# Keys turned by the DMA crossbar instead of TensorE, scores two slots behind the keys, sample states through ScalarE's queue

## What is computed

```python
def _retention(q, k, v, S0):            # chunks of 128 tokens
    ...
    def body(S, blk):
        qc, kc, vc = blk
        sc = jnp.einsum('bihd,bjhd->bhij', qc, kc) * decay
        o = (jnp.einsum('bhij,bjhv->bihv', sc, vc)
             + jnp.einsum('bihd,bhdv->bihv', qc, S) * q_dec[None, :, :, None])
        S = S * s_dec[None, :, None, None] + jnp.einsum('bjhd,bjhv->bhdv', kc * k_dec[None, :, :, None], vc)
        return S, o
...
def _layer(h, pos, S0, norm_g, w_in, w_out, ws, bs, ln_g, ln_b):
    xn = _rmsnorm(h, norm_g)
    proj = jnp.einsum('btd,de->bte', xn, w_in)
    q, k, v, g_r, u, v_g, g_g = jnp.split(proj, SPLITS, axis=-1)
    q = _rope(q.reshape(B, T, RET_HEADS, RET_DK), pos)
    k = _rope(k.reshape(B, T, RET_HEADS, RET_DK), pos) * (RET_DK ** -0.5)
    o, S = _retention(q, k, v, S0)
    o = o * lax.rsqrt(jnp.mean(o * o, axis=-1, keepdims=True) + EPS)
    o = o.reshape(B, T, RET_WIDTH).astype(h.dtype) * jax.nn.silu(g_r)
    ...
    m = u * s.astype(h.dtype) * jax.nn.silu(g_g)      # s: causal mix of the normed v_g in chunks of 128
    y = jnp.einsum('bte,ed->btd', jnp.concatenate([o, m], axis=-1), w_out)
    return h + y, S.astype(S0.dtype), vn
```

## Time and profile before

| | |
|---|---|
| median of 3 runs | 1146.09 us (1145.93 to 1146.74) |
| profiled execution, its own time | 1150.53 us |
| its span on the slowest core (core 7) | 1148.7 us |
| spans of all cores | 1139.2 to 1148.7 us |
| mean granted TensorE clock, cores | 0.998 to 0.999 of full speed |
| busy on core 7: PE, DVE, POOL, ACT | 1117.0, 789.0, 671.1, 635.7 us |
| chain that ended last, by engine | PE 90%, DMA 6%, issue, DVE, ACT and POOL 1% each |

### The profile page before, as it was taken

The page is one execution under the profiler, slowest core; times in us unless marked ns, Lnnn a source line. Parts: engine busy times, 40 slices in busy tenths (PEclk is TensorE's granted clock), DMA queues, the critical chain, the costliest instruction groups (busy, mean ns, idle before and its releaser), DMA issues.

```text
span 1148.7 us, 26973 instructions; the slowest of 8 cores (1139.2 to 1148.7 us)
## 1 busy us (share of the span) xinstructions
PE 1117.0 (97%) x8910; PEld 677.4 (59%) x8910; DVE 789.0 (69%) x1654; ACT 635.7 (55%) x1150; POOL 671.1 (58%) x704
## 2 busy tenths in 40 slices
PE   4999999999999999999989999999999999998997
PEld 2544566677667667545544446667667667664453
DVE  3775867777777777784574486777776777777854
ACT  3764856556556556524444487555555655662433
POOL 3267556667666666513476784666766766662332
PEclk9999999999999999999999999999999999999999
DMA  9831646546536555779680227346545546576553
GB/s 192 208 106 42 87 111 131 127 69 137 122 73 136 118 104 146 154 225 231 176 190 6 60 32 159 95 82 131 116 85 126 118 87 131 133 102 150 202 178 145
DMA packets 149720, 144.29 MB, mean 126 GB/s; under 512 B 46288, under 2 KB 119760, under 8 KB 149328
## 3 DMA queue, kind: packets, MB, share of 16 engines
q1 hardware_dynamic: 128320, 99.83, 31.2%
q0 software_dynamic: 21120, 42.48, 23.9%
q10 hardware_dynamic: 144, 0.26, 0.1%
HBM read 127.14 MB, written 44.24 MB: 149 GB/s over the span
## 4 chain that ended last, share of the span: by engine, by line
PE 90%; DMA 6%; issue 1%; DVE 1%; ACT 1%; POOL 1%; SPq 0%; DVEq 0%; ACTq 0%; POOLq 0%
PE ps L848 27%; PE ps L869 17%; PE ps L726 13%; PE ps L1292 13%; PE ps L657 4%; DMA cats<-catn 2%; PE ps L1228 2%; PE ps L949 1%; PE ps L1076 1%; PE ps L967 1%; PE ps L994 1%; PE ps L932 1%; DMA h<-hb_51 1%; PE ps L1034 1%; PE ps L997 1%
## 5 line engine op out<-in xcount | busy, mean ns | idle before, releaser
L848 PE MATMUL ps<-xnT,RW 128*128 128x512 bf16 x1536 | 359.6, 379 | 0.0
L848 PEld LDWEIGHTS ps<-xnT,RW 128*128 128x128 bf16 x1536 | 143.3, 98 | 141.4
L869 PE MATMUL ps<-RW,xnT 128*128 128x256 bf16 x1920 | 219.3, 272 | 0.0
L869 PEld LDWEIGHTS ps<-RW,xnT 128*128 128x128 bf16 x1920 | 184.1, 98 | 21.0
L897 POOL TENSOR_TENSOR kn<-A_k,B_k 128x512 bf16<-128x512 f32 x64 | 81.5, 1273 | 90.6 <-DVE B_k L893 52.8
L491 ACT ACT_TABLE_LOAD x73 | 93.7, 1283 | 44.7 <-DVE rs L1005 35.7
L491 ACT ACTIVATE B_q<-ps 64x512 f32<-64x512 f32 x128 | 75.8, 592 | 42.4 <-DVE A_q L906 36.7
L885 DVE SCALAR_TENSOR_TENSOR A_k<-ps,small,kr 128x256 f32<-128x256 f32 x128 | 56.1, 479 | 62.7 <-PE ps L869 52.5
L1015 POOL TENSOR_TENSOR catn<-og,rs 128x512 bf16<-128x512 f32 x64 | 66.0, 1045 | 41.6 <-ACT rs L491 31.1
L976 DVE SCALAR_TENSOR_TENSOR S_72<-S_72,ps 128x128 f32<-128x128 f32 x240 | 68.2, 284 | 17.4 <-DVE S_72 L976 2.9
L491 ACT ACTIVATE sgr_78<-ps 128x512 bf16<-128x512 f32 x32 | 19.1, 597 | 90.8 <-DVE B_k L893 87.1
(11 more groups left out here) (566 smaller groups left out, 2564.6 us busy)
## 6 DMA issues: line engine op xcount, KB each, us to landing
RW<-w_h POOLq DMA_DIRECT2D x80, 256.0 KB, 5.3
stt_124<-st SPq DMA_DIRECT2D x16, 512.0 KB, 5.2
stt_123<-st SPq DMA_DIRECT2D x16, 512.0 KB, 7.0
ss_out<-stt_123 SPq DMA_DIRECT2D x16, 512.0 KB, 4.1
ss_out<-stt_124 SPq DMA_DIRECT2D x16, 512.0 KB, 5.0
cats<-catn SPq DMA_DIRECT2D x28, 256.0 KB, 2.1
hb_49<-xp SPq DMA_DIRECT2D x6, 512.0 KB, 5.3
hb_50<-xp SPq DMA_DIRECT2D x6, 512.0 KB, 5.6
```

The source lines that it names most:

```text
L848: r = e.matmul(ps[:, b, :], w[:, k, :], xnT[:, k, s], start=(k == 0), stop=(k == 7))
L869: r = e.matmul(out(c).rearrange("p (g d) -> p g d", g=2), x, RW[:, 8 * sk + k:8 * sk + k + 9:8, :], start=(k == 0), stop=(k == 7))
```

## The change

The keys of units 0 to 30 in each layer (62 of 64) are no longer turned by PE. kn is written to DRAM (kd, 128 KB), from SP's queue, and a transposing DMA (the crossbar), also from SP, reads it into kT. The last unit of a layer keeps KT. kn and kT become two buffers each. SC and OO work for the unit two slots back, pp, and KV for the slot before, p. The gate's SiLU (GR) and the product for k32 (K32) become functions of their own. s32 takes the memory of sq. Of the state transfers, the loads for heads 1 to 7 and the stores for heads 0 to 6 are issued by ScalarE (28 and 28 in both layers), with slack 8.0 and 2.0. The turns of cats get a slack of 7.0 in all heads but the last. Behind the loop, the rest of units 30 and 31 is interleaved with the first products of the output projection. dma has a slack argument like dma_t's. The functions P_gg, P_q, P_u, GM and the sample group are otherwise as they were; KT, SC and KV index the two buffers by u.n % 2. DVE's and POOL's instructions are the same.

```diff
@@ Prog.schedule
-                free[e] = s + issue
+                free[e] = s + (0.4 if e == "act" else issue)
@@ build_nc
+    kd = nc.dram_tensor("kd", [H * NQ, 128, 512], BF16, kind="Internal").ap()
...
-        kT = T("kT", [128, 512], BF16)
-        kn = T("kn", [128, 4, 128], BF16)
+        kT = [T("kT%d" % i, [128, 512], BF16) for i in range(2)]
+        kn = [T("kn%d" % i, [128, 4, 128], BF16) for i in range(2)]
...
-        s32 = T("s32", [128, 512], F32)
+        s32 = T("s32", [128, 512], F32, at=sq.off)
...
+        LATER = 7.0
+
+        def dma_t(out, in_, r, w, key, nbytes, slack=0.0):
+            lastT[key] = i = P.add("sp", lambda e: e.dma_start_transpose(out=out, in_=in_), r, w, semkey=key, nbytes=2.5 * nbytes,
                                after=[lastT[key]] if key in lastT else ())
+            P.ops[i].slack = slack
@@ P_kgr
-            act(t[:].rearrange("p (c d) -> p c d", c=4), kg[:, :, 1, :], AF.Silu, [], t.k() + kb, 512, tset="silu")
-            pool(lambda e: e.tensor_tensor(out=kn[:], in0=a3, in1=b3, op=ALU.add), A_k.k() + B_k.k(), kn.k(), 512)
+            kn_ = kn[u.n % 2]
+            pool(lambda e: e.tensor_tensor(out=kn_[:], in0=a3, in1=b3, op=ALU.add), A_k.k() + B_k.k(), kn_.k(), 512)
+            if u.n < H * NQ - 1:
+                dma("sp", kd[u.n], kn_[:].rearrange("p c d -> p (c d)"), kn_.k(), [("kd", u.n)], kn_.name, 131072)
...
+        def GR(l, u):
...
+        def K_turn(l, u):
+            t = kT[u.n % 2]
+            dma_t(t[:].rearrange("p (c i) -> p c i", c=4), kd[u.n], [("kd", u.n)], t.k(), "kT", 131072)
+
         def KT(l, u):
...
+        def K32(l, u):
...
@@ OO
                 dma_t(VO[:, h, t0:t0 + n * 512].rearrange("p (c i) -> p c i", c=4 * n), src,
-                      names, VO.k(h, (t0, t0 + n * 512)), "catT", 131072 * n)
+                      names, VO.k(h, (t0, t0 + n * 512)), "catT", 131072 * n, LATER if h < H - 1 else 0.0)
@@ s_load
-            dma("sp", t[:], st_in[l, half * 8:half * 8 + 8, h].rearrange("b d v -> d b v"), [], t.k(), t.name, 524288, after=after)
+            dma("act" if h else "sp", t[:], st_in[l, half * 8:half * 8 + 8, h].rearrange("b d v -> d b v"), [], t.k(),
+                (t.name, "l", min(h, 1)), 524288, after=after, slack=8.0 if h else 0.0)
@@ s_kv
-                    dma("sp", ss_out[l, half * 8:half * 8 + 8, h].rearrange("b d v -> d b v"), t[:], t.k(), [("sso", l, h, half)], t.name, 524288)
+                    dma("act" if h < H - 1 else "sp", ss_out[l, half * 8:half * 8 + 8, h].rearrange("b d v -> d b v"), t[:], t.k(), [("sso", l, h, half)], (t.name, "s", h < H - 1), 524288, slack=2.0)
@@ the loop over units
+                if pp:
+                    SC(l, pp)
                 P_kgr(l, u)
+                P_gg(l, u)
+                if pp:
+                    OO(l, pp)
+                GR(l, u)
+                P_q(l, u)
                 if p:
-                    SC(l, p)
-                P_q(l, u)
+                    KV(l, p)
+                if u.q == 3:
+                    next(kv)
+                P_u(l, u)
                 if u.q == 3:
                     next(kv)
                 if p:
                     GM(l, p)
-                P_gg(l, u)
-                if p:
-                    OO(l, p, pp)
-                if u.q == 3:
-                    next(kv)
-                for f in (KT, P_u) if p else (P_u, KT):
-                    f(l, u)
+                if n < H * NQ - 1:
+                    K_turn(l, u)
+                if u.q == 0:
+                    K32(l, u)
...
-                KV(l, u)
@@ behind the loop
-            o_front(l, 0, 0, 4)
+            SC(l, pp)
+            KT(l, p)
+            GM(l, p)
+            o_front(l, 0, 0, 1)
+            OO(l, pp)
+            KV(l, p)
+            o_front(l, 0, 1, 2)
             SC(l, p)
-            GM(l, p)
-            OO(l, p, pp)
+            o_front(l, 0, 2, 4)
+            OO(l, p)
```

More of the change, by code:

```diff
@@ L498, in pool, with dma @@
             P.add("pool", fn, r, w, t_pool(n))
-        def dma(eng, out, in_, r, w, key, nbytes, after=(), **kw):
-            return P.add(eng, lambda e: e.dma_start(out=out, in_=in_, **kw), r, w, semkey=key, nbytes=nbytes, after=after)
+        def dma(eng, out, in_, r, w, key, nbytes, after=(), slack=0.0, **kw):
+            i = P.add(eng, lambda e: e.dma_start(out=out, in_=in_, **kw), r, w, semkey=key, nbytes=nbytes, after=after)
+            P.ops[i].slack = slack
+            return i
         lastT = {}
-        def dma_t(out, in_, r, w, key, nbytes):
-            lastT[key] = P.add("sp", lambda e: e.dma_start_transpose(out=out, in_=in_), r, w, semkey=key, nbytes=2.5 * nbytes,
+        LATER = 7.0
+        def dma_t(out, in_, r, w, key, nbytes, slack=0.0):
+            lastT[key] = i = P.add("sp", lambda e: e.dma_start_transpose(out=out, in_=in_), r, w, semkey=key, nbytes=2.5 * nbytes,
                                after=[lastT[key]] if key in lastT else ())
+            P.ops[i].slack = slack
         def ld(t, src, nbytes=65536, **kw):
@@ L858, in P_kgr @@
             w, w2 = W(l, u.h, "k"), W(l, u.h, "gr")
-            t = sgr[u.n % 2]
             kb = [bk(b) for b in KG]
@@ L900, in P_kgr @@
                      A_k.k() + B_k.k(), ra2.k(), 128)
+        def GR(l, u):
+            t = sgr[u.n % 2]
+            kg = ps[:, KG[0]:KG[1] + 1, :].rearrange("p b (c g d) -> p (b c) g d", c=2, g=2)
+            act(t[:].rearrange("p (c d) -> p c d", c=4), kg[:, :, 1, :], AF.Silu, [], t.k() + [bk(b) for b in KG], 512, tset="silu")
         def P_q(l, u):
@@ L931, in tr @@
                 for c in range(4):
-                    r = e.transpose(pb[:, c * 128:(c + 1) * 128], kn[:, c, :], identb[:])
+                    r = e.transpose(pb[:, c * 128:(c + 1) * 128], kn[u.n % 2][:, c, :], identb[:])
                 return r
[L934 to L939, removed]
+            pe(tr, kn[u.n % 2].k() + identb.k(), [bk(b)], 4 * SM)
+            t = kT[u.n % 2]
+            act(t[:], pb[:, 0:512], AF.Copy, [], t.k() + [bk(b)], 512)
+        def K32(l, u):
+            b2 = brot()
+            pe(lambda e: e.matmul(ps[:, b2, 0:32], ra2[:], identf[:, 0:32], start=True, stop=True), ra2.k() + identf.k(), [bk(b2)], 0.09)
+            dve(lambda e: e.tensor_copy(k32[:], ps[:, b2, 0:32]), [], k32.k() + [bk(b2)], 32)
         def SC(l, u):
             b = brot()
-            a, t, o = kT, qT[u.n % 2], scT
+            a, t, o = kT[u.n % 2], qT[u.n % 2], scT
             first = u.q == 0
@@ L960, in KV @@
             b = brot()
-            a = kn
+            a = kn[u.n % 2]
             h = u.h
@@ L982, in KV, with OO @@
             act(t[:], S32[:], AF.Copy, S32.k(), t.k(), 512)
-        def OO(l, u, prev):
+        def OO(l, u):
             b = brot()
@@ L1477, in build_nc @@
                 units.append(u)
-            tail_fill = []
             def slot(n):
```

## The result

The changed kernel takes 1198.37 us (median of 4 runs, 1194.85 to 1200.87), the kernel before 1146.41 in the same sessions: a ratio of 1.0449, 95% interval 1.042 to 1.0479, so 4.5% slower where 0.8% faster was forecast. The profiled execution's slowest core is again core 7.

The account below looks back on a forecast made before the run. PE was taken to bound the kernel, busy 1117.0 of 1148.7 us. The terms −13.6 + 2 + 2 = −9.6 us took the profiled 1150.5 to 1140.9, and 4.4 less for the median gave 1136.5 us, range 1131.0 to 1147.0.

Parts of the forecast that it names:

- PE, removed: On PE, 62 of 64 key transpositions go, at 0.22 us each: −13.6 us.
- Neither is on the path: On ACT, 37.1 us of copies removed and 20.7 us of state transfers added cost 0, ACT working 46.11 of 80 us.
- So inside the loop: 0.: In the head loop, key write and turn take 9.9 us together against 9.7 to 11.4 available, so cost 0.
- the slowest I found there: Mid-loop transfers of twice the size, 4.7 and 5.2 us, taken as measure for the key's write and turn.
- Scores at the two layer ends: At both layer ends, scores wait for late key write and turn: +2 us, between 0 and 19.4.
- output weights: In layer 1, PE's 2.3 us wait for wo_6 may go or stay: 0, between −2.3 and 0.
- the slower rival: Keys late at the layer ends: 19.4 us of waits there instead of 2, giving 1153.9 us; chance 0.20.
- But they stood behind a 256 KB turn: At layer ends, slow key-sized transfers followed a 256 KB turn that the new order moves back; supports +2 of 19.4.
- Start of layer 0's output projection: Before layer 0's first pair product, hb loads go behind stores, some 5.5 us later: +2 us, between 0 and 5.5.
- the sum: Whole kernel: −13.6 + 2 + 2 = −9.6 us, giving a forecast of 1136.5 us.
- Keys late at the layer ends: At layer ends, scores of unit 30 or cats turns wait 19.4 us instead of 2: 1153.9 us; chance 0.20.

Follow-up runs that it names:

- e8: The change with all state transfers back on SP's queue: 1165.3 us, ratio 1.0176 to the kernel before.
- e12: The kernel before with the state transfers on ScalarE's queue as in the change, keys on TensorE: 1157.2 us, ratio 1.0091.
- e10: The change with states on SP's queue, units 26 and 27's turn early, last stores at slack 30, each head's first-quarter keys on TensorE: 1141.6 us, ratio 0.9951.
- e13: The change with slack 60 for the last head's two state stores alone, the turn of units 26 and 27 left late: 1216.0 us, ratio 1.0536.
- e6: The change with the keys of each head's first quarter turned by TensorE, one slot later: 1167.8 us, ratio 1.0214.

## Why the prediction was wrong, point by point

- **PE, removed: −13.6 us.** Right. 0.22 us per transposition in e8's layer 1, as put, and key blocks of successive heads stand 41.7 us apart on the change's core 1 where nothing disturbs (41.6 expected).
- **ACT: "Neither is on the path", "Cost 0".** Not so in e12, where ScalarE's queue costs 10.4 us. A share of 46 in 80 us said nothing of when the engine is free: a gate's SiLU that comes a little late holds back the next block of keys. In the change itself PE waits 0.9 us for it, so this is not what turned the result.
- **"So inside the loop: 0."** The step that failed is the choice of rows. 4.7 and 5.2 us were "the slowest I found there", from transfers of the old order; the change brings its own traffic to the same place, a state load of 13.2 us beside a turn of 10.9. Write and turn then took 4.8 and 10.9, 15.7 in all, where the text had 9.7 to 11.4 to spare. Such waits took 17.1 us in place of 0.
- **Scores at the two layer ends, +2; output weights, 0.** The place of the slower rival was right, the waiting work was not: scores of unit 30 were on time, and the output weights, costed between −2.3 and 0, took 28.2 us. The failed step is "But they stood behind a 256 KB turn … which the new SP order puts behind the turn of unit 30". It was read as relief. The new order sets that turn between the two state stores. What a turn can do in company was in the trace of before already and was not used: a 128 KB turn issued at 475.23, behind both stores, took 11.6 us, and in layer 1 wo_4 took 16.5 us beside a 256 KB turn of 15.5 (issues 1011.63 and 1011.44). One row was also misread: the turn of 8.0 us, issued at 454.13, is layer 0's 256 KB turn itself (units 26 and 27), ahead of the write at 457.43. The write's own turn, at 462.70, took 4.4, so layer 0 had 9.5 us in place of 13.1.
- **Start of layer 0's output projection, +2.** PE's wait for hb_51 is 2.2 us.
- **Not in the sum at all:** at six of these waits PE's granted clock goes down to 0.50, the lower level (as from 498 to 506). PE's busy time grew by 1.7 us instead of falling by 13.6. 27.6 us of it lie at the lower level, which costs 13.8 of these 15.3. With it the slowest core's account nearly closes: −13.6 + 17.1 (keys) + 25.7 (weights, 28.2 less 2.5 before) + 13.8 (clock) + 2.4 (B_q) + 2.2 (hb_51) is 47.6 of the 49.1 us.
- **The rivals.** Keys late at the layer ends was priced at 1153.9 and decided at 11.6 us of waits; 45 us of waits came, most of it of another kind. The Trainium skill's rule ("VectorE: DVE Perf Modes", Rules for kernel authors), TensorE for a 128×128 transpose when PSUM will do, held for the change as made. e10, with 46 of 64 key blocks through the crossbar, is 0.5% faster than the kernel that follows it. So crossbar turns came out either way here, by what was in flight beside them.

## What to carry to other kernels

Work taken off the bounding engine and given to DMA is worth its time only if the transfer lands in the traffic that the change itself makes: read landing times at the place where it will be issued, with what will be in flight there, and not where the old order was quiet. A delay that a planner puts on a transfer moves it next to something else; look at its new neighbours in each queue at both ends of the loop. Move one transfer at a time, and look up which tiles share its memory before moving a store.

## What the runs showed of the hardware that was not expected

A crossbar turn beside weight loads can keep the DMA engines counted as busy (share 1.00 to 1.80) while they move 21 to 78 GB/s, with 512 KB state stores in flight (the change) or without (e13, core 1). The same kind of mixture moved 186 to 218 GB/s in e6, and in the middle of the loop of the kernel before, with no weight load in flight, a 256 KB turn between two such stores landed in 3.8 us (issue 429.50). What in the mixture does it was not tried: the weight loads were never taken away. And a stall costs time behind it as well: after the one of 4.12 us the key block took 5.01 us in place of 3.66, with a mean granted clock of 0.71 from 243.8 to 249.6.
